# A new order of work on three engines in the odd layer of an encoder

## The chip, the cores and the metric

The kernel runs on one core of one Trainium2 chip, in one launch. The metric is the device time of that launch in microseconds (us), lower is better. A run gives one time; a profiled execution gives a trace as well, with its own span from the first to the last instruction. TensorE (PE) multiplies, ScalarE (ACT) and VectorE (DVE) work on its results, and SyncE (SP) issues the transfers.

## The reference

The program is a two-layer encoder trunk over x of 512 x 1024, float32: an even layer (differential attention beside a gated recurrence), then the odd layer, then a final RMS norm. The change touches only the odd layer:

```python
h = rmsnorm(x, norm_w)
qc, kc, vc, gc = split_cols(h @ w_in, (2048, 256, 256, 2048))
oc = window_gqa_with_sink(qc, kc, vc, sink, cos, sin) * silu(gc)
x = x + oc @ w_out
```

The attention has 32 query heads of 64 features that share 4 key heads; each query sees keys at most 128 positions away, and each head has a learned sink logit in its softmax:

```python
s = q @ k.T / 8, masked to |i - j| <= 128
m = max(max(s), sink)
p = exp(s - m); p = p / (sum(p) + exp(sink - m))
o = p @ v
```

## The kernel before

All float32 products are made from split parts: a matrix w becomes `w_hi` (rounded, by ScalarE: `high`) and `w_lo` (the rest, by VectorE: `low`), and each product is three matmuls, lines 73 to 75. Everything is kept transposed, features on the partitions, 512 tokens along the free dimension.

The odd layer has eight iterations `h` (`HEADS`), and each has two half-steps, `half` 0 and 1. A half-step treats two query heads: their scores against the window, in four tiles `t` of 128 queries, for the two heads `a` side by side. Iteration 0 is written out, iterations 1 to 6 are a loop, iteration 7 is written out again. Each engine runs its own program, written out by hand in `half_step`, and they meet only at semaphores; each engine works strictly in the order written. That order is what the change alters.

What a half-step does, by the names in the code:

- `proj(h, n)` on TensorE: 24 matmuls that project 128 columns of `w_in`. n = 1 and 3 give queries, 2 and 4 give gates. Two banks `PB` take them in turns. Each is issued as two parts of 12, with other work between. `rotate` (VectorE, six operations) reads a query projection, `silu` (ScalarE, line 1523) a gate projection into `gate[:, half]`; both free the bank.
- `scores(t)` on TensorE into banks `S`; `maxima(t)` on VectorE (two reductions, line 1648, and a small operation, line 1652); `soft_max(t)` on ScalarE (line 1483, exp, two times); `turns(t)`: TensorE transposes the probabilities into banks `T` (line 1309); `high_turn(t)` (ScalarE, line 1490) and `low_turn(t)` (VectorE, line 1659) split them into `probsT`; `values(t)` multiplies with v into bank `O` (line 1323). There is one `probsT`, so `values(t)` must wait for `low_turn(t)`. Tile 3 of a half-step is finished in the next one, which begins with `turns(.., 3)`.
- After two tiles `swap_halves` (ScalarE, lines 1502 and 1503) and `add_halves` (VectorE, lines 1690 and 1692) put the two heads' results together.
- The row sums: `exp_sink` and `weigh` make 1 / sum, `spread_weight` (ScalarE, line 1495) widens it to 64 columns, `turn_weight` (TensorE, line 1333) transposes it into bank `W`, `apply_weight` multiplies by the gate (line 1697), `scale_y` by the result (line 1704). `high_y` and `low_y` split this into y.
- `out_tile(j)` on TensorE: six matmuls of the output projection of the iteration before, into the same single bank `W`; `add_out` on VectorE (line 1716) adds it to the residual `xT` and frees W. There are four tiles per half-step, and `out_tile(j)` waits for `add_out` of tile j - 1. Iteration 0 has none.
- The weights: SP loads n = 3, 4, 5, 6 of each iteration into four slots (`load`), and the out weights (`load_out`). `high` and `low` split n = 3 to 6 for use in this and the next iteration, `high_out` and `low_out` the out weights. A load waits for the low part that last read its slot; loads 5 and 6 stand in SP's queue behind the moves of the rotated queries of half 1, the out weights behind these.

Silu needs another function table on ScalarE than exp, and each change of table is an instruction of 1.28 us. In the odd layer before, these loads stand right in front of the activation that needs them, at lines 1523 and 1483.

The order in a half-step before, where it matters: ScalarE ends a half-step with `soft_max` 3, `exp_sink` and the silu of the gate that TensorE made in this half-step. VectorE makes a `low` between `add_halves` and `add_out` of tile 1, and a second one behind `add_out` of tile 2. TensorE has `turn_weight` between the two parts of its first projection.

## Time and profile before

| | us |
|---|---|
| three runs | 1277.93, 1285.24, 1282.14 |
| median | 1282.14 |
| the profiled execution | 1286.09 |
| its span | 1284.3 |
| TensorE busy | 1166.4 (91%) |
| VectorE busy | 965.6 (75%) |
| ScalarE busy | 653.3 (51%) |
| mean granted TensorE clock | 0.971 of full |

The odd layer's half-steps fill the stretch from about 805 to 1250 us of the span. The profiled execution's own time is 1.8 us above its span, and 4 us above the median of the three runs. Busy shares are means over stages with different limits; a busy TensorE is one that has a matmul in flight.

### The profile page before, as it was taken

What the parts mean: (1) busy time and instruction counts of PE and PEld (TensorE: products, weight loads), DVE (VectorE), ACT (ScalarE), POOL (GpSimd) and SP (SyncE); (2) the same over time, 40 slices, a digit from 0 to 9 for tenths busy, and PEclk for the clock granted to TensorE, in tenths of its full rate; (3) what the DMA queues carried; (4) which work ended last, traced back from release to release, by engine and by line L of the source; (5) the groups of instructions that cost most, each with busy time, mean ns of one, the idle gap of its engine ahead of it and who ended that gap; (6) DMA issues with size and microseconds to landing.
All of it is one profiled execution on the core that took longest, in us unless ns stands there. A gap on an engine that the chain in (4) does not pass through costs nothing. (4 is left out here: it accounts for less than half of the span.)

```text
span 1284.3 us, 18420 instructions
## 1 busy us (share of the span) xinstructions
PE 1166.4 (91%) x5708; PEld 931.0 (72%) x5708; DVE 965.6 (75%) x1891; ACT 653.3 (51%) x1246; POOL 0.2 (0%) x4
## 2 busy tenths in 40 slices
PE   5989999999999999999999769889898888989975
PEld 3767778777787787787777547767777777777754
DVE  6677779778788797787787857567777777777764
ACT  5364463553645545535445433565556565555652
POOL 0000000000000000000000000000000000000000
PEclk8999999999999999999999879989999999999998
DMA  6521522315215115233151005412132321213201
GB/s 184 148 66 50 144 69 67 114 49 131 65 43 137 49 50 146 65 80 100 49 131 34 17 25 128 131 51 82 50 101 72 89 82 50 83 49 88 70 7 66
DMA packets 131096, 103.06 MB, mean 80 GB/s; under 512 B 5360, under 2 KB 116336, under 8 KB 131056
## 3 DMA queue, kind: packets, MB, share of 16 engines
q1 hardware_dynamic: 131056, 102.54, 29.2%
q8 instruction: 23, 0.38, 0.1%
q14 instruction: 17, 0.14, 0.0%
HBM read 77.36 MB, written 2.10 MB: 62 GB/s over the span
## 5 line engine op out<-in xcount | busy, mean ns | idle before, releaser
L73 PE MATMUL bank_proj<-hH,w_hi 128*128 128x512 f32 x576 | 229.9, 399 | 4.3 <-DVE hL L139 4.3
L75 PE MATMUL bank_proj<-hH,w_lo 128*128 128x512 f32 x576 | 225.8, 392 | 0.0
L74 PE MATMUL bank_proj<-hL,w_hi 128*128 128x512 f32 x576 | 225.5, 391 | 0.0
L73 PEld LDWEIGHTS bank_proj<-hH,w_hi 128*128 128x128 f32 x576 | 109.0, 189 | 26.5 <-issue 5.1
L75 PEld LDWEIGHTS bank_proj<-hH,w_lo 128*128 128x128 f32 x576 | 108.8, 189 | 23.7
L74 PEld LDWEIGHTS bank_proj<-hL,w_hi 128*128 128x128 f32 x576 | 109.1, 189 | 21.6
L73 PE MATMUL bank_odd_proj<-hH,w_hi 128*128 128x512 f32 x288 | 118.8, 412 | 5.1 <-DVE hL L139 4.4
L1483 ACT ACTIVATE probs<-bank_odd_score,small 128x256 f32<-128x256 f32 (+1 forms) x128 | 66.4, 524 | 105.7 <-DVE small L1652 105.4
L74 PE MATMUL bank_odd_proj<-hL,w_hi 128*128 128x512 f32 x288 | 114.2, 396 | 0.0
L75 PE MATMUL bank_odd_proj<-hH,w_lo 128*128 128x512 f32 x288 | 114.2, 396 | 0.0
L968 DVE TENSOR_TENSOR w_lo<-w_raw,w_hi 128x1024 fp32r<-128x1024 f32 x73 | 89.0, 1220 | 20.1 <-ACT w_hi L565 20.0
L565 ACT ACTIVATE w_hi<-w_raw 128x1024 fp32r<-128x1024 f32 x75 | 78.6, 1051 | 39.9 <-DMA w_raw<-in_w_in_even 36.3
L612 ACT ACTIVATE probs<-bank_score,small 128x512 f32<-128x512 f32 x64 | 43.5, 684 | 95.5 <-DVE small L818 95.5
L1490 ACT ACTIVATE probsT<-bank_odd_turn 128x256 fp32r<-128x256 f32 (+1 forms) x128 | 49.0, 435 | 74.0 <-PE bank_odd_turn L1309 74.0
L1659 DVE TENSOR_TENSOR probsT<-bank_odd_turn,probsT 128x256 fp32r<-128x256 f32 (+1 forms) x128 | 56.9, 486 | 37.4 <-ACT probsT L1490 37.3
L465 PE MATMUL bank_score<-scaled 128*128 128x128 f32 x448 | 61.0, 287 | 10.5 <-DVE attT L984 8.9
L73 PE MATMUL bank_odd_wide<-y,o_hi 128*128 128x512 f32 x112 | 49.4, 441 | 22.5 <-DVE xT L1716 21.8
L668 ACT ACTIVATE scaled<-decay 128x1024 f32<-128x1024 f32 x32 | 33.9, 1059 | 70.4 <-PE bank_score L465 68.6
L465 PEld LDWEIGHTS bank_score<-scaled 128*128 128x128 f32 x448 | 57.7, 200 | 16.2 <-issue 7.1
L73 PEld LDWEIGHTS bank_odd_proj<-hH,w_hi 128*128 128x128 f32 x288 | 55.7, 193 | 16.4 <-DVE hL L139 5.5
L1294 PE MATMUL bank_odd_score<-ks,qs 128*128 128x256 f32 (+1 forms) x256 | 65.1, 359 | 0.0
L75 PEld LDWEIGHTS bank_odd_proj<-hH,w_lo 128*128 128x128 f32 x288 | 55.0, 191 | 12.3
(229 smaller groups left out, 2439.8 us busy)
## 6 DMA issues: line engine op xcount, KB each, us to landing
w_raw<-in_w_in_even SPq DMA_DIRECT2D x72, 512.0 KB, 4.4
w_raw<-in_w_in_odd SPq DMA_DIRECT2D x36, 512.0 KB, 4.5
qs<-parts SPq DMA_DIRECT2D x96, 128.0 KB, 2.3
ks<-parts SPq DMA_DIRECT2D x40, 256.0 KB, 4.2
o_raw<-in_w_out_even SPq DMA_DIRECT2D x16, 512.0 KB, 4.9
o_raw<-in_w_out_odd SPq DMA_DIRECT2D x14, 512.0 KB, 6.5
out<-w_raw SPq DMA_DIRECT2D x4, 512.0 KB, 2.7
mixT<-in_x SPq DMA_DIRECT2D x2, 512.0 KB, 5.5
```

Source lines behind the costliest of these rows:

```text
L73: pe.matmul(out, hi, moving_hi, start=start, stop=False)
L74: pe.matmul(out, hi, moving_lo, start=False, stop=False)
L75: return pe.matmul(out, lo, moving_hi, start=False, stop=stop)
L465: mm = pe.matmul(S[l % 2][:, c * P:(c + 1) * P], scaled[:, l % 2, 0, c * P:(c + 1) * P], scaled[:, l % 2, 1, c * P:(c + 1) * P], start=Tru ...
L565: act.activation(w_hi[s][:], w_raw[s][:], ACT.Copy).then_inc(w_high.sem, 1)
L612: act.activation(probs[:, c], S[c][:], ACT.Exp, bias=neg_max[:, i:i + 1], scale=SCALE, accum_out=row_sum[:, i:i + 1]).then_inc(S[c].free.s ...
L668: act.activation(scaled[:, l % 2], buf(l)[:, :, :], ACT.Exp).then_inc(near_exp.sem, 1)
L968: dve.tensor_tensor(w_lo[s][:], w_raw[s][:], w_hi[s][:].bitcast(F32), ALU.subtract).then_inc(w_low.sem, 1)
L1294: mm = pe.matmul(at, query, keys, start=part == 0, stop=False)
L1483: act.activation(probs[:, t % 2, a, 0:n * P], S[a][:, 0:n * P], ACT.Exp, bias=neg_max[:, i:i + 1], scale=SCALE, accum_out=row_sum[:, i:i + ...
L1490: act.activation(probsT[:, 0, 0:n, a], chunked(T[a][:, 0:n * P]), ACT.Copy).then_inc(probs_high[a].sem, 1)
L1659: dve.tensor_tensor(probsT[:, 1, 0:n, a], chunked(T[a][:, 0:n * P]), probsT[:, 0, 0:n, a].bitcast(F32), ALU.subtract).then_inc(T[a].free.s ...
```

## The change

It moves calls within `half_step` on the three engines. No operation of the attention or the projections is added or left out. What moves:

- TensorE: `turn_weight` from between the two parts of the first projection to behind `scores` 1.
- ScalarE: the silu of a gate moves from the end of its half-step to the next one, behind `swap_halves`; an explicit load of the exp table stands behind `high_turn` 0. `high_y` 0 moves to the beginning of the next iteration's half 0. Both `high_out` stand in front of `soft_max` 0 in half 0; `high` 4 and `high` 5 stand in front of `soft_max` 0 in half 1; `high` 3 and `high` 6 stand behind `soft_max` 1.
- VectorE: `apply_weight` and `scale_y` move behind `maxima` 1. `low` 4 and `low` 5 stand at the beginning of half 1, around `add_halves`; `low` 3 and `low` 6 stand between `add_out` 2 and `add_out` 3. Nothing but `add_halves` is left between `add_out` 0 and 1. `maxima` 3 comes before `low_turn` 2. `rotate` comes before `low_y` 1.

```diff
--- before.py
+++ after.py
@@ -1378,11 +1378,12 @@
                     proj(h, n, 0)
                 if not first:
                     values(h_before, before, 3, group if half else group_before)
-                    turn_weight(h_before, before, turn_of(half, outs))
                 if project:
                     proj(h, n, 1)
                 turns(h, half, 0)
                 scores(h, half, 1)
+                if not first:
+                    turn_weight(h_before, before, turn_of(half, outs))
                 if project:
                     proj(h, n + 1, 0)
                 values(h, half, 0, group)
@@ -1517,9 +1518,8 @@
 
                 bank, use = bank_of(n)
                 act.wait_ge(bank.full.sem, bank.full.at(h, use))
-                if not zeroth:
-                    if W.free.due(h, turn_of(n // 4, True)):
-                        act.wait_ge(W.free.sem, W.free.at(h, turn_of(n // 4, True)))
+                if n == 2 and not zeroth:
+                    act.wait_ge(W.free.sem, W.free.at(h, turn_of(0, True)))
                 act.activation(gate[:, half], bank[:], ACT.Silu).then_inc(bank.free.sem, 1)
 
             nrm.highs(act)
@@ -1549,37 +1549,37 @@
 
             def half_step(h, half, zeroth, last):
                 before, h_before = 1 - half, (h if half else h - 1)
-                n = 3 + 2 * half
                 first, outs = zeroth and not half, not zeroth and not half
                 if not first:
                     high_turn(h_before, before, 3)
                 if outs:
+                    high_y(h - 1, 0)
                     high_out(h - 1, 0)
+                    high_out(h - 1, 1)
+                if half:
+                    high(h, 4)
+                    if not last:
+                        high(h, 5)
                 soft_max(h, half, 0)
                 if not first:
                     spread_weight(h_before, before)
-                if outs:
-                    high_out(h - 1, 1)
-                if not first:
                     swap_halves(h_before, before, 1)
-                if not last or not half:
-                    high(h, n)
+                    silu(h_before, 4 - 2 * half, half, zeroth)
                 high_turn(h, half, 0)
+                act.preload_act_table_set(EXP_LOG)
+                soft_max(h, half, 1)
+                if not half:
+                    high(h, 3)
+                elif not last:
+                    high(h, 6)
                 if outs:
                     high_y(h - 1, 1)
-                soft_max(h, half, 1)
-                if not last or not half:
-                    high(h, n + 1)
                 high_turn(h, half, 1)
                 soft_max(h, half, 2)
                 swap_halves(h, half, 0)
                 high_turn(h, half, 2)
                 soft_max(h, half, 3)
                 exp_sink(h, half)
-                if not (last and half):
-                    silu(h, 2 + 2 * half, 1 - half, zeroth and not half)
-                if half:
-                    high_y(h, 0)
 
             def iteration(h, zeroth, last):
                 half_step(h, 0, zeroth, last)
@@ -1590,6 +1590,7 @@
                 iteration(h, False, False)
             iteration(HEADS - 1, False, True)
             high_turn(HEADS - 1, 1, 3)
+            high_y(HEADS - 1, 0)
             spread_weight(HEADS - 1, 1)
             swap_halves(HEADS - 1, 1, 1)
             high_y(HEADS - 1, 1)
@@ -1742,44 +1743,45 @@
             def half_step(h, half, zeroth, last):
                 before, h_before = 1 - half, (h if half else h - 1)
                 first, use = zeroth and not half, turn_of(half, not zeroth)
-                lows = not (last and half)
+                out = lambda j: zeroth or add_out(h, [4 * half + j], 5 * half + 2 + j)
                 if not first:
                     low_turn(h_before, before, 3)
                 maxima(h, half, 0)
                 if not first:
                     weigh(h_before, before)
-                if not half and not first:
-                    low_y(h - 1, 0)
+                if half:
+                    low(h, 4)
+                elif not first:
                     low_out(h - 1, 0)
                     low_out(h - 1, 1)
+                    low_y(h - 1, 0)
                 if not first:
                     add_halves(h_before, before, 1)
+                if half and not last:
+                    low(h, 5)
+                low_turn(h, half, 0)
+                maxima(h, half, 1)
+                if not first:
                     apply_weight(h, before, use)
                     scale_y(h_before, before, h, use)
-                low_turn(h, half, 0)
-                maxima(h, half, 1)
+                if not (last and half):
+                    rotate(h, 2 * half + 1)
                 if not half and not first:
                     low_y(h - 1, 1)
-                if not (last and half):
-                    rotate(h, 2 * half + 1)
                 low_turn(h, half, 1)
                 maxima(h, half, 2)
-                if not zeroth:
-                    add_out(h, range(4 * half, 4 * half + 1), 5 * half + 2)
+                out(0)
                 add_halves(h, half, 0)
-                if lows:
-                    low(h, 3 + 2 * half)
-                if not zeroth:
-                    add_out(h, range(4 * half + 1, 4 * half + 2), 5 * half + 3)
+                out(1)
+                maxima(h, half, 3)
                 low_turn(h, half, 2)
-                maxima(h, half, 3)
+                out(2)
                 shift_sink(h, half)
-                if not zeroth:
-                    add_out(h, range(4 * half + 2, 4 * half + 3), 5 * half + 4)
-                if lows:
-                    low(h, 4 + 2 * half)
-                if not zeroth:
-                    add_out(h, range(4 * half + 3, 4 * half + 4), 5 * half + 5)
+                if not half:
+                    low(h, 3)
+                elif not last:
+                    low(h, 6)
+                out(3)
 
             def iteration(h, zeroth, last):
                 half_step(h, 0, zeroth, last)
```

## Rows read from the trace of the kernel before

A row of a timeline is: start in us, duration in us, engine, line, operation, tiles, count, and in brackets the idle time before it with what ended it.

**Rows 1.** TensorE's waits, 835 to 1254 us: line and tile, releaser, total us, times, longest.

```profile
PE bank_odd_wide L73 <- DVE xT L1716: 21.8, 31, 1.2
PE bank_odd_wide L1333 <- ACT spread L1495: 12.1, 10, 1.7
PE bank_odd_out L1323 <- DVE probsT L1659: 7.1, 5, 2.9
PE bank_odd_turn L1309 <- ACT probs L1483: 2.3, 3, 1.0
```

**Rows 2.** Timeline of TensorE over one iteration.

```profile
1000.85 0.60 PE L1309 MATMUL bank_odd_turn<-eye,probs 128*128 128x128 f32 x4
...
1008.40 0.60 PE L1309 MATMUL bank_odd_turn<-eye,probs 128*128 128x128 f32 x4
...
1009.82 0.47 PE L73 MATMUL bank_odd_proj<-hH,w_hi 128*128 128x512 f32 x1
...
1015.87 0.82 PE L1309 MATMUL bank_odd_turn<-eye,probs 128*128 128x128 f32 x6
...
1022.67 0.23 PE L1296 MATMUL bank_odd_score<-band,eye_b 128*128 128x128 bf16 x1
1024.08 0.50 PE L73 MATMUL bank_odd_wide<-y,o_hi 128*128 128x512 f32 x1 [1.18 <-DVE xT L1716]
...
1025.59 0.88 PE L1323 MATMUL bank_odd_out<-probsT,v 128*128 128x256 f32 x6
1026.88 0.47 PE L73 MATMUL bank_odd_wide<-y,o_hi 128*128 128x512 f32 x1 [0.41 <-DVE xT L1716]
...
1028.34 0.60 PE L1309 MATMUL bank_odd_turn<-eye,probs 128*128 128x128 f32 x4
...
1034.52 0.63 PE L1333 MATMUL bank_odd_wide<-eye,spread 128*128 128x128 f32 x4 [1.62 <-ACT spread L1495]
...
1057.76 0.60 PE L1309 MATMUL bank_odd_turn<-eye,probs 128*128 128x128 f32 x4
```

**Rows 3.** Timeline of ScalarE, same iteration, around the two changes of table.

```profile
999.47 1.28 ACT L1523 ACT_TABLE_LOAD   x1
1000.77 0.60 ACT L1523 ACTIVATE gate<-bank_odd_proj 128x512 f32<-128x512 f32 x1
...
1031.54 1.28 ACT L1483 ACT_TABLE_LOAD   x1 [0.63 <-DVE small L1652]
...
1034.27 1.05 ACT L1474 ACTIVATE o_hi<-o_raw 128x1024 fp32r<-128x1024 f32 x1
```

**Rows 4.** Timeline of VectorE in half 1 of that iteration.

```profile
1016.92 1.02 DVE L1659 TENSOR_TENSOR probsT<-bank_odd_turn,probsT 128x384 fp32r<-128x384 f32 x2 [1.70 <-ACT probsT L1490]
...
1022.08 1.23 DVE L1723 TENSOR_TENSOR w_lo<-w_raw,w_hi 128x1024 fp32r<-128x1024 f32 x1
1023.34 0.69 DVE L1716 TENSOR_TENSOR xT<-xT,bank_odd_wide 128x512 f32<-128x512 f32 x1
1023.95 1.02 DVE L1659 TENSOR_TENSOR probsT<-bank_odd_turn,probsT 128x384 fp32r<-128x384 f32 x2
1024.88 0.75 DVE L1648 TENSOR_REDUCE small<-bank_odd_score 128x1 f32<-128x256 f32 x2
1025.66 0.16 DVE L1652 SCALAR_TENSOR_TENSOR small<-small,neg_sink 128x2 f32<-128x2 f32 x1
```

**Rows 5.** TensorE's waits, 860 to 1227.6 us.

```profile
PE bank_odd_wide L1333 <- ACT spread L1495: 9.2, 7, 1.6
```

**Rows 6.** SP's issues around load 5, and the page's row on landing.

```profile
1048.18 1.09 SPq L1190 DMA_DIRECT2D w_raw<-in_w_in_odd  x2
...
w_raw<-in_w_in_odd SPq DMA_DIRECT2D x36, 512.0 KB, 4.5
```

**Rows 7.** One stretch: busy us (instructions) of five engines, granted clock, DMA share, GB/s.

```profile
853.00:863.00 10.00, 7.89 (x29) 6.43 (x30) 7.11 (x17) 6.95 (x15) 0.00 (x0) 0.66 0.02 5
```

**Rows 8.** Table loads of the even layer's preload, by line.

```profile
L719 ACT ACT_TABLE_LOAD x8 | 10.3, 1283 | 0.1
```

## The prediction, made before the changed kernel was run

> **What bounds the kernel now.** I read four views. The page's busy line first: TensorE is busy 91% of the span, so what can be won is its idle time and its slow clock. Then the waits of TensorE over the part that the change touches: four waits, 21.8 + 12.1 + 7.1 + 2.3 = 43.3 us [rows 1]. Then TensorE in order of time for one iteration, to see where in a half-step each gap falls, and ScalarE and VectorE at the same places [rows 2 to 4].
>
> I call the start of `turns(.., 3)` time 0 of a half-step. Half 1 starts at 1000.85 and ends at 1028.34 (27.5 us), half 0 ends at 1057.76 (29.4 us) [rows 2]. Their TensorE work is the same; the 1.9 us between them is mostly one gap, 1.62 us before the transposes of the spread sums. Both halves have a gap of 1.18 us before `out_tile` 2 and of 0.41 before `out_tile` 3. These gaps count from the modelled end of a matmul; the next one may start before that end. So I reckon from start to start, which makes a gap some 0.17 us more: half 1's first out matmul at 1024.08 could have started at 1022.73, 0.06 behind the last of `scores` 3 (1022.67).
>
> **Gap 1, the spread sums (half 0).** ScalarE converts one out weight, loads the exp table (1031.54, after waiting for VectorE), does `soft_max` 0 and then the spread [rows 3]. TensorE has only half a projection and `values` 3 to cover that. After the change `turn_weight` stands behind `scores` 1. Working forward for the new half 0, by the durations in these rows and the starts in the same view: `high_turn` 3 at 0.42 to 0.95; `high_y` 0.5, to 1.5; two `high_out` of 1.05 (1034.27), to 3.6; `soft_max` 0 takes 0.9, to 4.5, with no table load in it; spread 0.5, to 5.0; the two halves of the swap 0.8, to 5.8; table load 1.28 and silu 0.5, to 7.6. `turn_weight` now comes at 8.6: without it, and with the two halves of the projection set together, `turns` 0 starts at 7.2 (in half 1 it is at 1008.40 with 0.35 us of those transposes ahead), and `scores` 1 end 1.4 later (1008.40 to 1009.82). The spread is 3.6 us early. The wait goes whole: 9.2 us in the seven half-0 steps from 860 to 1227.6 [rows 5].
>
> **What of the silu hides.** It frees the bank that `proj(n+1)` writes, at 9.0; silu ends at 7.6, so 1.3 us are over. It also stands before `high_turn` 0, whose input is there at 7.2 + 0.41 = 7.6 (two transposes' time and the signal): no delay, and no slack. In half 1 `high` 4 and `high` 5 take the place of the out weights (ends 3.1), `soft_max` 0 ends at 4.0, the swap waits for `values` 3 until 4.6 as before and the silu ends near 7.2. The exp load, now behind `high_turn` 0, lies at 8.2 to 9.5; `soft_max` 1 can start at about 9.9, since VectorE must reduce `scores` 1 first. It costs nothing. As many loads as before (two a half-step), each at a place where ScalarE idled.
>
> **Gaps 2 and 3, the low parts.** `out_tile` 2 waits for `add_out` 1 on VectorE, and that stands behind a 1.23 us low part (1022.08, then 1023.34) [rows 4]. With `low` gone from there, `add_out` 1 starts at 1022.1, and its result is seen at 1022.83, against the 1022.73 at which TensorE could go on. Gap 2 shrinks to 0.1. Next `values` 2 needs `low_turn` 2, which now stands behind `maxima` 3. From 1022.7: two reductions 0.75 (the second not before 1022.95, when its scores are whole), the small operation 0.16 and its start delay, to 1023.75; `low_turn` 2 takes 0.93 (1023.95 to 1024.88), seen by TensorE at 1024.70. `out_tile` 2 ends its issue at 1022.83 + 1.51 = 1024.34 (1.51 is 1024.08 to 1025.59). So a **new wait of 0.36 us** per half-step appears before `values` 2; bounds: 0, if the reductions overlap more, and 0.91, if all of `maxima` 3 were exposed; I take 0.36, for its terms are rows. `add_out` 2 then runs from 1024.7 to 1025.4, before `values` 2 has issued at 1025.42, so gap 3 goes whole, and `out_tile` 3 takes 1.46: the half-step ends at 1026.88 where it ended at 1028.34 [rows 2], **1.46 us** sooner. The one low part left runs at 24.5 to 25.7 of the half-step; the next projection wants it at 27, and `add_out` 3, behind it, has its input at 26.2.
>
> **VectorE's first part.** Half 0: `low_turn` 3, `maxima` 0 and `weigh` to 3.0, two `low_out` of 1.2, to 5.3, `low_y` to 5.9; then the swap is just ready, `add_halves` to 6.8, `low_turn` 0 at 8.06 (`turns` 0 + 0.83), `maxima` 1 to 9.9. `apply_weight` and `scale_y`, 1.55 with their wait, now sit between this and `rotate` (4.0), then `low_y` 0.6: 16.1. `low_turn` 1 can start at 15.05 + 1.05 = 16.1 (1015.87 to 1016.92 is that 1.05) [rows 2, 4]. Exactly on time. In half 1 there is no `low_y`, and the old idle of 1.70 at 1016.92 becomes 0.55. I charge 0, with bounds 0 and 0.5 us per half 0.
>
> **Weight loads.** SP's waits are for `rotate` and for low parts that all end no later than now, so the loads start within 1 us of the same place. But `high` 5 is wanted sooner: load 5 is issued 2.8 us behind the rotation's end (1048.18), so at 18.3, lands 4.5 later at 22.8 [rows 6], and is read at 28.0. 5 us are over.
>
> **First and last iteration.** In iteration 0 no output tiles cover VectorE; the 7.1 and 2.3 us of [rows 1] lie mostly there. `values` 2 waits 2.9 twice; its chain (softmax 2, swap, `add_halves`, a low part) loses 1.23 and gains `maxima` 3, 0.91: 0.3 better twice. `turns` 3 no longer waits for `soft_max` 3 (0.5), nor `turn_weight` for the spread (0.3). About 1.4 us. TensorE ran at the lower of its two levels for part of this: over 853 to 863 its granted clock is 0.66 of full, after such a wait [rows 7]. Whether a wait of 2.6 instead of 2.9 spares that is open: between 0 and 5 us gained; I take 1. The last half-step has no projections: there silu and both loads fall into a chain of latencies, to about 7.2 for `high_turn` 0, but VectorE's `maxima` 1 comes where it came (8.9), as it had `apply_weight` and `scale_y` ahead before. With the spread's 1.7 partly gone and this, 0.5 gained (bounds: 2 lost, 2 gained).
>
> **Sum.** From 860 to 1227.6 there are six half-1 steps and seven half-0 steps: 13 x 1.46 = 19.0 for gaps 2 and 3 less the new wait; gap 1, 9.2, and start to start 7 x 0.17 = 1.2 more; half 0's first `out_tile` waits stay. That is 29.4. Then 1.4 + 1 + 0.5. Together **32 us**. The profiled execution took 1286.1 (span 1284.3), so 1254; it stands 4 us above the median of the three runs (1282.1). Against the median: **1250**.
>
> The Trainium skill (ScalarE: Activation LUTs, What ACT_TABLE_LOAD costs) counts a drain of about 1.38 us with every 1.28 us load. The trace shows the silu starting 1.30 us after its load began, with nothing between, at 999.47 and 1000.77 [rows 3], so it isn't in my sum; it is the second rival.
>
> **Rivals.**
> (a) VectorE becomes the bound. For: in the new half 0 nothing is over before `low_turn` 1, and from there `maxima` 2, `soft_max` 2, the swap, `add_halves` and `add_out` 1 follow without slack to `out_tile` 2. Each microsecond late comes back whole. Against: half 1 has 0.55 over. At 0.8 us in 13 half-steps, 10 us: 1260.
> (b) A table load costs more than its row when ScalarE has work queued on either side. For: in the old order its neighbours were often waits. Against: the silu's load shows none [rows 3]. Were 1.3 us paid behind each, the silu ends at 8.9 in half 0 and `high_turn` 0 is 1.3 late; in half 1 0.3 after slack: 7 x 1.3 + 6 x 0.3 = 11 us, 1261. This is what the Trainium skill's drain would make.
> (c) A load that is not wanted appears: the first exp of the loop gets one of its own, since silu ran before it elsewhere. The Trainium skill (ScalarE: Activation LUTs, Table sets: the hidden batching unit) says that a compiler pass puts a load before every activation that needs one. Against: the even layer loads by an explicit preload (line 719) in each of its 8 turns, and its exps at the loop's top show no load of their own [rows 8]. Price: 1.28 before `soft_max` 0 of half 0 pushes silu and `high_turn` 0 by as much, 7 x 1.28 = 9: 1259.
> (d) **Slower**: ScalarE stands at `high` 5 for a weight that hasn't landed, with `soft_max` 0 of half 1 queued behind it, and so spread, swap, silu and the whole half-step. It was behind `soft_max` before, in a gap. The slack is 5.2 us and an iteration gains 4.5 (29.4 over 6.5 of them), so it decides from a load 9.7 us late, 14 us instead of 4.5 to land; at 17 us the loss is 2.8 net in each of 7 iterations: 1282 + 20 = 1302. Against it: nothing else is on the queue then but the small q moves and the out weights behind it.
> (e) The gaps are only passed on, TensorE's idle returning elsewhere: within 0.5% (6 us, about what this kernel's measurement can tell from no change). It would need 2 us of new wait per half-step (26 over 13); no step above is over by so much.
>
> **Chances.** Forecast 0.70 (own range 1243 to 1257), (a) 0.12, (b) 0.05, (c) 0.05, (d) 0.03, (e) 0.05. All of the forecast, (a), (b) and (c) are faster by over 0.5%, 0.92; same 0.05; slower 0.03. The low end takes the slow clock of the first iteration as spared (4 us more) and the new wait at nothing (13 x 0.36 = 5, of which I count half, since both ends rarely meet): 1243. The high end reaches past (a) to (c), 1264.
>
> **What would show it.** The transposes from `spread` with no wait before them; no wait of TensorE on `xT` over 0.3 us; a new one on `probsT` before `values` 2 of 0.1 to 0.5 us, some 13 times; half-steps of 26.0 to 26.3 us, both alike; table loads still 16 and 16, now under lines of silu and preload, the first exp with one of its own at most once. Wrong: waits on `xT` of 1 us left, or the projection waiting for the silu, or half 0 longer than half 1 by over 0.5.

## The result, and the profile after

| | before | after |
|---|---|---|
| median of four runs, us | 1282.01 | 1248.3 |
| lowest and highest | 1277.93 to 1285.24 | 1245.95 to 1249.27 |
| the profiled execution, and its span | 1286.09, 1284.3 | 1248.77, 1247.0 |
| from TensorE's first `scores` to the end of the span | 475.97 | 444.27 |

The ratio is 0.9736, with a 95% interval of 0.9705 to 0.9767: 33.7 us by the medians, where 32 were forecast. The two spans differ by more, 37.3 us, and 5.65 us of that lie ahead of the first `scores` (808.35 against 802.70), in code that the change does not touch. The part that it touches gave 31.7. In the tables below I therefore count from the first `scores` of each trace.

TensorE's waits in the changed kernel from 800 to 1220 us, which is its odd layer but for the very end; columns as in [rows 1]:

```profile
PE bank_odd_out L1323 <- DVE probsT L1660: 12.9, 21, 2.5
PE bank_odd_turn L1309 <- ACT probs L1484: 3.3, 4, 1.0
PE bank_odd_wide L1333 <- ACT spread L1496: 1.0, 1, 1.0
PE bank_odd_wide L73 <- DVE xT L1717: 0.6, 4, 0.2
```

[Rows 1] begin at 835 us, 27 us into the odd layer. Over the part that corresponds to the one above, 805 to 1254 us, the kernel before has the same two first lines, 3.1 us on `probs`, and on `probsT`:

```profile
PE bank_odd_out L1323 <- DVE probsT L1659: 10.4, 7, 2.9
```

The 21.8 us on `xT` of [rows 1] are 0.6; the 12.1 on the spread are 1.0, one wait behind the last half-step. What grew is the wait on `probsT`, 10.4 to 12.9. Of its 21 waits, 14 are the new short one before `values` 2 (0.17 to 0.30 us each); the other 7, in the first iteration and the last half-step, have their counterparts in the kernel before.

TensorE over one iteration, half 0 from 1007.17 to 1033.21 and the half 1 ahead of it from 981.13 (a row: start us, us, engine, line, operation, tiles, count, idle before and its releaser):

```profile
981.13 0.60 PE L1309 MATMUL bank_odd_turn<-eye,probs 128*128 128x128 f32 x4
...
989.69 0.61 PE L1333 MATMUL bank_odd_wide<-eye,spread 128*128 128x128 f32 x4
...
1002.95 0.23 PE L1296 MATMUL bank_odd_score<-band,eye_b 128*128 128x128 bf16 x1
1003.10 0.50 PE L73 MATMUL bank_odd_wide<-y,o_hi 128*128 128x512 f32 x1
...
1004.98 0.96 PE L1323 MATMUL bank_odd_out<-probsT,v 128*128 128x256 f32 x6 [0.23 <-DVE probsT L1660]
```

```profile
1005.77 0.40 PE L73 MATMUL bank_odd_wide<-y,o_hi 128*128 128x512 f32 x1
...
1007.17 0.60 PE L1309 MATMUL bank_odd_turn<-eye,probs 128*128 128x128 f32 x4
...
1015.73 0.61 PE L1333 MATMUL bank_odd_wide<-eye,spread 128*128 128x128 f32 x4
...
1031.03 0.95 PE L1323 MATMUL bank_odd_out<-probsT,v 128*128 128x256 f32 x6 [0.17 <-DVE probsT L1660]
...
1033.21 0.60 PE L1309 MATMUL bank_odd_turn<-eye,probs 128*128 128x128 f32 x4
```

Both half-steps take 26.04 us, where [rows 2] had 27.5 and 29.4. The transposes of the spread sums (989.69, 1015.73) wait for nothing. `out_tile` 2 starts at 1003.10, 0.15 behind the last of `scores` 3, `values` 2 waits 0.23 (0.17 in half 0), and `out_tile` 3 follows at 1005.77 without a wait.

ScalarE in half 0, for [rows 3], and VectorE at the places of [rows 4]:

```profile
1008.65 2.01 ACT L1475 ACTIVATE o_hi<-o_raw 128x1024 fp32r<-128x1024 f32 x2
1010.55 0.47 ACT L1484 ACTIVATE probs<-bank_odd_score,small 128x256 f32<-128x256 f32 x1
...
1011.45 0.64 ACT L1496 ACTIVATE spread<-small 128x512 f32<-128x512 f32 x1
...
1012.91 1.28 ACT L1523 ACT_TABLE_LOAD   x1
1014.21 0.60 ACT L1523 ACTIVATE gate<-bank_odd_proj 128x512 f32<-128x512 f32 x1
1014.70 0.66 ACT L1491 ACTIVATE probsT<-bank_odd_turn 128x256 fp32r<-128x256 f32 x2
1015.38 1.28 ACT L1569 ACT_TABLE_LOAD   x1
1017.03 0.58 ACT L1484 ACTIVATE probs<-bank_odd_score,small 128x384 f32<-128x384 f32 x1 [0.37 <-DVE small L1653]
```

```profile
997.20 1.02 DVE L1660 TENSOR_TENSOR probsT<-bank_odd_turn,probsT 128x384 fp32r<-128x384 f32 x2 [0.72 <-ACT probsT L1491]
...
1002.36 0.69 DVE L1717 TENSOR_TENSOR xT<-xT,bank_odd_wide 128x512 f32<-128x512 f32 x1
1002.96 0.75 DVE L1649 TENSOR_REDUCE small<-bank_odd_score 128x1 f32<-128x256 f32 x2
...
1003.82 1.01 DVE L1660 TENSOR_TENSOR probsT<-bank_odd_turn,probsT 128x384 fp32r<-128x384 f32 x2
...
1022.44 0.69 DVE L1710 TENSOR_TENSOR y<-gated,y 128x512 fp32r<-128x512 f32 x1
1023.24 1.02 DVE L1660 TENSOR_TENSOR probsT<-bank_odd_turn,probsT 128x384 fp32r<-128x384 f32 x2
```

`high_turn` 0 takes over from the silu at 1014.70, which is 7.53 us into the half-step (from 1007.17), with no idle time, as worked out (7.6). The exp load (1015.38) stands 8.2 us into it and `soft_max` 1 9.9, both as forecast. `maxima` 3 (1002.96) comes before `low_turn` 2 (1003.82). `low_turn` 1 comes at 1023.24 behind `low_y` at 1022.44 with nothing between (16.07, forecast 16.1); in half 1 there is an idle 0.72 instead of the 1.70 of [rows 4]. The function table is loaded 16 times for the silus and 16 times by the explicit preload, and one first exp has a load of its own:

```profile
L1523 ACT ACT_TABLE_LOAD x16 | 20.5, 1283 | 0.3
L1569 ACT ACT_TABLE_LOAD x16 | 20.5, 1283 | 0.3
...
L1484 ACT ACT_TABLE_LOAD x1 | 1.3, 1283 | 0.0
```

Where the 31.7 us came from, by stretches that begin and end with `turns(.., 3)`:

| stretch | before | after | gained | forecast |
|---|---|---|---|---|
| iteration 0, from the first `scores` | 47.70 | 46.25 | 1.45 | 2.4 |
| 13 half-steps up to the last | 371.59 | 340.49 | 31.10 | 29.4 |
| the last half-step | 22.51 | 23.39 | -0.88 | 0.5 with the end |
| from its `turns` 3 to the end | 34.17 | 34.14 | 0.03 | |
| sum | 475.97 | 444.27 | 31.70 | 32.3 |

### The profile page after: what moved, and what is told of

Same layout as the page of the kernel before. It is cut to its first block and busy times, and to the rows that moved or that the text cites. A ratio compares the mean times of both kernels' runs of the same rounds, so it can differ in the third digit from the quotient of the medians.

```text
span 1247.0 us, 18415 instructions
## 1 busy us (share of the span) xinstructions
PE 1158.3 (93%) x5708; PEld 926.6 (74%) x5708; DVE 961.7 (77%) x1891; ACT 653.4 (52%) x1247; POOL 0.2 (0%) x4
## 5 line engine op out<-in xcount | busy, mean ns | idle before, releaser
L968 DVE TENSOR_TENSOR w_lo<-w_raw,w_hi 128x1024 fp32r<-128x1024 f32 x73 | 88.8, 1217 | 19.8 <-ACT w_hi L565 19.8
L1660 DVE TENSOR_TENSOR probsT<-bank_odd_turn,probsT 128x256 fp32r<-128x256 f32 (+1 forms) x128 | 57.0, 485 | 28.3 <-ACT probsT L1491 27.5
L1323 PEld LDWEIGHTS bank_odd_out<-probsT,v 128*128 128x128 f32 x320 | 45.9, 192 | 23.0 <-issue 16.5
```

Source lines behind the costliest of these rows:

```text
L968: dve.tensor_tensor(w_lo[s][:], w_raw[s][:], w_hi[s][:].bitcast(F32), ALU.subtract).then_inc(w_low.sem, 1)
L1323: mm = pe.matmul(at, value, probsT[:, part, j].rearrange("p a q -> p (a q)"), start=j == 0 and part == 0, stop=j == n - 1 and part == 1)
L1660: dve.tensor_tensor(probsT[:, 1, 0:n, a], chunked(T[a][:, 0:n * P]), probsT[:, 0, 0:n, a].bitcast(F32), ALU.subtract).then_inc(T[a].free.s ...
```

## The experiments

Ten kernels ran, each beside the kernel before on the same chip. Two theories stood against each other throughout. One, by slack: an edit is worth what it takes off the path that ends last, and what it puts on it, and much of it lies beside other work. The other, by gaps: an edit is worth the gap that it was made for.

The two half-steps in the table are those of one iteration near 1000 us.

| kernel | median, us | half 1, half 0, us | iteration 0 | 13 half-steps | last half-step |
|---|---|---|---|---|---|
| before | 1282.0 | 27.5, 29.4 | 47.70 | 371.59 | 22.51 |
| changed | 1248.3 | 26.04, 26.04 | 46.25 | 340.49 | 23.39 |
| e1, `turn_weight` back | 1254.2 | 26.18, 27.02 | 46.22 | 346.71 | 23.45 |
| e2, `turn_weight` alone | 1278.9 | 28.05, 28.51 | 47.06 | 370.64 | 23.02 |
| e3, low parts back | 1269.6 | 27.27, 27.28 | 49.79 | 356.62 | 23.47 |
| e4, `low_turn` 2 first | 1245.2 | 25.96, 26.05 | 45.03 | 338.71 | 22.83 |
| e5, silu back | 1246.1 | 26.09, 26.04 | 46.22 | 340.74 | 20.63 |
| e6, filler on VectorE | 1250.1 | 26.04, 26.46 | 46.24 | 343.07 | 22.18 |
| e7, one more table load | 1255.6 | 26.04, 27.26 | 46.20 | 347.17 | 23.15 |
| e8, round trip filled | 1233.1 | 25.2, 25.6 | 42.11 | 330.71 | 23.02 |
| e10, last silu back | 1246.7 | 26.02, 26.02 | 46.20 | 340.32 | 20.62 |
| e9, e8 and the last half | 1231.4 | 25.2, 25.6 | 42.09 | 330.63 | 20.96 |

**e1: `turn_weight` back between the parts of the projection.** On the changed kernel:

```diff
                     values(h_before, before, 3, group if half else group_before)
+                    turn_weight(h_before, before, turn_of(half, outs))
...
                 scores(h, half, 1)
-                if not first:
-                    turn_weight(h_before, before, turn_of(half, outs))
```

> The changed kernel, but turn_weight stands between the two parts of the first projection again, as before the change. Nothing else is undone. Theory (slack): the table load is no longer ahead of the spread, so the spread is ready 4.9 us into half 0 and 4.4 into half 1, and TensorE comes to it at 4.4: a wait of 0.5 to 0.7 us in half 0 and under 0.15 in half 1, 7 x 0.6 + 6 x 0.1 = 5 us: 1253. Rival (the move of turn_weight is what removed gap 1): the wait of 1.6 us per half 0 comes back whole, 11 us: 1259 to 1260.

1254.23 us, ratio to before 0.9799 (0.9772 to 0.9827); 6.2 us more than the changed kernel over the 13 half-steps. The spread is waited for by 0.53 us in half 0, not by the 1.62 of [rows 2], as the theory by slack has it. What neither had: in half 0 a second wait, before `out_tile` 1, and a half 1 that is 0.14 us longer.

```profile
1012.58 0.63 PE L1333 MATMUL bank_odd_wide<-eye,spread 128*128 128x128 f32 x4 [0.53 <-ACT spread L1495]
...
1023.30 0.82 PE L1309 MATMUL bank_odd_turn<-eye,probs 128*128 128x128 f32 x6
...
1027.57 0.47 PE L73 MATMUL bank_odd_wide<-y,o_hi 128*128 128x512 f32 x1 [0.30 <-DVE xT L1716]
```

From `turns` 0 to `turns` 1 it is 7.46 us again (1015.84 to 1023.30), in the changed kernel 7.90 (1014.29 to 1022.19). With the transposes between them, VectorE has 0.4 us more for its chain from `low_turn` 0 to `low_turn` 1, which was exactly on time. So the move of `turn_weight` is worth 6.2 us of the 13 half-steps. By the waits in half 0, 0.53 + 0.17 from start to start is 7 x 0.7 = 5 of them, an estimate, and a high one, since the first half 0 takes 28.08 us in both kernels. I put the rest down to the stretch in which VectorE was tight and which the move lengthens; no run shows that part by itself. What took the wait from 1.62 to 0.53 is the load and the order on ScalarE together; no run divides these two.

**e2: `turn_weight` alone, on the kernel before.**

```diff
-                    turn_weight(h_before, before, turn_of(half, outs))
...
                 scores(h, half, 1)
+                if not first:
+                    turn_weight(h_before, before, turn_of(half, outs))
```

> The kernel before, with one edit of the change alone: turn_weight behind scores 1. Theory (slack): gap 1 goes (1.8 us from start to start per half 0), but VectorE's apply_weight, which still stands before low_turn 0 and maxima 1, now waits for the transposes until 9.0 us into the half-step, so low_turn 0 ends at 11.2 instead of 9.1, rotate ends at 16.4 in half 1 and 17.0 in half 0, and low_turn 1 is 0.3 and 0.9 us late; that comes back before out_tile 2. 7 x (1.8 - 0.9) - 6 x 0.3 = 4.5 us gained: 1277.5. Rival (the edit is worth its gap): 7 x 1.7 = 12 us gained, 1270.

1278.92 us, ratio 0.9989 (0.9974 to 1.0005): no clear change. The 13 half-steps are 0.95 us shorter. A steady half 0 gained 0.8 where 0.9 were expected, half 1 lost 0.5 instead of 0.3. The wait on `xT` from 860 to 1220 us, columns as in [rows 1]:

```profile
PE bank_odd_wide L73 <- DVE xT L1717: 30.7, 39, 1.4
```

The spread's 9.2 us of [rows 5] are gone, and the wait on `xT` took nearly all of them (21.8 in [rows 1]): `apply_weight`, still ahead of `low_turn` 0, holds VectorE until the late transposes are done. By itself the edit is worth nothing. That its partner on VectorE (`apply_weight` behind `maxima` 1) would be enough to free its 6.2 us is likely by e1, but the two were not run as a pair.

**e3: the low parts back in their gaps.** On the changed kernel:

```diff
                 add_halves(h, half, 0)
+                if not (last and half):
+                    low(h, 3 + 2 * half)
                 out(1)
...
+                if not (last and half):
+                    low(h, 4 + 2 * half)
                 out(3)
```

with `low` 4 and 5 gone from the beginning of half 1, and on ScalarE `high(h, 3 + 2 * half)` and `high(h, 4 + 2 * half)` both behind `soft_max` 1.

> The changed kernel, with the low parts back in their old gaps on VectorE (one between add_halves and add_out 1, one before add_out 3), and the two high parts they need both behind soft_max 1 on ScalarE. maxima 3 stays before low_turn 2. Theory (slack): add_out 1 is 1.23 us later, TensorE had 0.1 us over it, all behind it is late by the same: half-steps of 27.2 instead of 26.04, 13 x 1.15 = 15 us: 1263. Rival (gaps 2 and 3 are both the low parts' work and the new wait stays on top): 13 x 1.8 = 24 us: 1272.

1269.55 us, ratio 0.9915 (0.9888 to 0.9941). A steady half-step is 1.27 us longer (27.30 on the mean, 26.03 in the changed kernel), about one low part of [rows 4], 16.1 us over the 13, and iteration 0 is 3.5 us longer, which the expectation left out; together 19.8 from the first `scores` on. The short wait before `values` 2 stayed as it was (waits from 860 to 1208 us):

```profile
PE bank_odd_wide L73 <- DVE xT L1712: 15.9, 16, 1.2
PE bank_odd_out L1323 <- DVE probsT L1655: 2.7, 13, 0.2
```

This is the largest single part of the change: 19.8 of 31.7 us. With the 6.2 of e1 that is 26.0; what makes up the other 5.7 no run shows.

**e4: `low_turn` 2 before `maxima` 3 again.**

```diff
-                maxima(h, half, 3)
                 low_turn(h, half, 2)
+                maxima(h, half, 3)
                 out(2)
```

> The changed kernel with one pair exchanged on VectorE: low_turn 2 before maxima 3 again. Theory (slack): the new wait before values 2 (0.2 us from the modelled end, 0.3 from start to start) goes; soft_max 3 is 0.9 us later, still 1 us before turns 3 need it; add_out 2 comes 0.1 late at most. Half-steps of 25.75 instead of 26.04, 13 x 0.27 = 3.5 us gained: 1245. Rival (VectorE is the bound here, so the order is indifferent and the wait moves to out_tile 3): same, 26.0 per half-step.

1245.18 us, ratio 0.9732 (0.9708 to 0.9757). The wait before `values` 2 went, but a half-step behind the first gained 0.04 us on the mean, not 0.27: the theory by slack, as I had filled it in, failed, and the first rival is right about the half-steps. The wait moved to `out_tile` 3. TensorE and VectorE at that place:

```profile
999.39 0.50 PE L73 MATMUL bank_odd_wide<-y,o_hi 128*128 128x512 f32 x1
...
1000.88 0.88 PE L1323 MATMUL bank_odd_out<-probsT,v 128*128 128x256 f32 x6
1001.92 0.47 PE L73 MATMUL bank_odd_wide<-y,o_hi 128*128 128x512 f32 x1 [0.16 <-DVE xT L1717]
```

```profile
999.25 1.01 DVE L1660 TENSOR_TENSOR probsT<-bank_odd_turn,probsT 128x384 fp32r<-128x384 f32 x2
...
1001.09 0.69 DVE L1717 TENSOR_TENSOR xT<-xT,bank_odd_wide 128x512 f32<-128x512 f32 x1
```

`add_out` 2 (1001.09) can't start before `out_tile` 2's last matmul is done, and takes 0.69; so two out tiles can't follow each other within about 2.5 us (999.39 to 1001.92), while the tile and `values` 2 between them issue in 2.2. That round trip through the single bank W holds `out_tile` 3. VectorE's own work would hold it as well: `maxima` 3 is done at 1001.12, the last matmul of `out_tile` 2 at 1001.04, so at this place the two limits can't be told apart. At `out_tile` 1 of half 0, which waits 0.16 us too, they can: VectorE is free 0.1 us before `add_out` 0 starts (1021.71, the last matmul of `out_tile` 0 ends at 1021.68), and the two tiles stand 2.49 us apart (1020.05 to 1022.54). The median is 3.1 us below the changed kernel's. In the traces 3.7 us are gained, and they lie in iteration 0 (1.2), in the 13 half-steps (1.8, over half of it in the first of them, which runs partly at the lower clock) and in the last half-step (0.6).

**e5: the silu back at the end of its half-step.**

```diff
-                    silu(h_before, 4 - 2 * half, half, zeroth)
                 high_turn(h, half, 0)
-                act.preload_act_table_set(EXP_LOG)
...
                 exp_sink(h, half)
+                if not (last and half):
+                    silu(h, 2 + 2 * half, 1 - half, zeroth and not half)
```

The silu's own wait for W stands as in the kernel before.

> The changed kernel, with the silu back at the end of its own half-step and the exp table loaded where soft_max 0 needs it; all else as changed. Theory (slack): in half 0 soft_max 0 comes 1.3 us later, behind the load, the swap ends at 7.1 instead of 5.8, but high_turn 0 has its input only at 7.5 and turn_weight comes at 8.6: nothing on TensorE's path moves, half-steps of 26.0 to 26.1, 1248 to 1250. Rival (the silu's move is what took the load off the spread's path, and is worth its 1.3 us per half 0): 7 x 1.3 = 9 us more, 1257.

1246.14 us, ratio 0.9734 (0.9698 to 0.9771), its interval over that of the changed kernel. The 13 half-steps are 0.25 us longer, so the move of the silu, taken from the finished order, is worth nothing there: the first theory held and the rival's 9 us did not come. But the last half-step takes 20.63 us instead of 23.39. ScalarE in that half-step, in the changed kernel and in e5:

```profile
1194.28 1.28 ACT L1523 ACT_TABLE_LOAD   x1
1195.58 0.60 ACT L1523 ACTIVATE gate<-bank_odd_proj 128x512 f32<-128x512 f32 x1
1196.07 0.65 ACT L1491 ACTIVATE probsT<-bank_odd_turn 128x256 fp32r<-128x256 f32 x2
```

```profile
1193.77 0.66 ACT L1491 ACTIVATE probsT<-bank_odd_turn 128x256 fp32r<-128x256 f32 x2
```

`high_turn` 0 comes 6.6 us into the half-step in the one and 5.8 in the other (from 1189.44 and 1187.98): with no projection for TensorE, silu and load stand in a chain of latencies. But that chain is the smaller part of the difference, as e10 shows below.

**e6: a filler before `rotate`.**

```diff
                 if not (last and half):
+                    dve.tensor_reduce(filler[:, half:half + 1], rope[:, 0], AX_X, ALU.max)
                     rotate(h, 2 * half + 1)
```

> The changed kernel with one more operation on VectorE in front of each rotate, a reduction of 512 columns whose result nobody reads, some 0.65 us. Theory (VectorE's chain to low_turn 1 is exactly on time in half 0): half 1 has 0.72 us over and stays at 26.0; half 0 has 0.15 to 0.2 over and becomes 26.5, 7 x 0.47 = 3.3 us: 1251.5. Rival (VectorE is the bound throughout, so each half-step pays): 13 x 0.65 = 8.5 us: 1257. Rival (TensorE alone is the bound): nothing, 1248.

1250.14 us, ratio 0.9753 (0.9718 to 0.9787). The filler takes 0.68 us. Half 0 grew by 0.42 us, half 1 by nothing, as the theory by slack had it (0.47 and 0); over the 13 half-steps it is 2.6 us, where 3.3 were expected. So the idle 0.72 us in half 1 are real slack, and half 0 has some 0.25.

**e7: one more table load before `soft_max` 0 of half 0.**

```diff
                     high_out(h - 1, 1)
+                    act.preload_act_table_set(EXP_LOG)
```

> The changed kernel with one more load of the exp table on ScalarE, in front of soft_max 0 of half 0 (1.28 us, 7 times on the path from 860 us on). Theory (nothing is over on the way silu, high_turn 0, low_turn 0, rotate, low_turn 1): half 0 grows by 1.1 to 1.3 us, half 1 not; 7 x 1.2 = 8.5 us: 1257. Rival (a load costs a drain beside its row): 7 x 2.5 = 17 us, 1265. Rival (ScalarE is idle half the time, so a load hides): 1248.

1255.63 us, ratio 0.9805 (0.9768 to 0.9841). Half 0 takes 27.26 us, 1.22 more, the row's 1.28 less a little; half 1 stays at 26.04. 6.7 us over the 13 half-steps, where 8.5 were expected: the first half 0 of them, which runs in part at the lower clock, grew by nothing (27.74 us, in the changed kernel 28.08). So this load costs its row and nothing beside it, and in a steady half 0 it comes back whole. TensorE's `turns` 3 at the two ends of a half 0 (the half 1 behind it ends at 1063.11):

```profile
1009.82 0.60 PE L1309 MATMUL bank_odd_turn<-eye,probs 128*128 128x128 f32 x4
...
1037.08 0.60 PE L1309 MATMUL bank_odd_turn<-eye,probs 128*128 128x128 f32 x4
```

**e8: work for TensorE in W's round trip.** On top of e4, the two projections of a half-step cut differently, and the silu table loaded ahead of `high_turn` 0:

```diff
-                    proj(h, n, 1)
+                    proj(h, n, tiles=range(4, 7))
                 turns(h, half, 0)
                 scores(h, half, 1)
+                    proj(h, n, tiles=range(7, 8))
                     turn_weight(h_before, before, turn_of(half, outs))
...
-                    proj(h, n + 1, 1)
+                    proj(h, n + 1, tiles=range(4, 6))
                 turns(h, half, 1)
...
                 values(h, half, 1, group)
+                    proj(h, n + 1, tiles=range(6, 7))
...
                 values(h, half, 2, group)
+                    proj(h, n + 1, tiles=range(7, 8))
...
+                    act.preload_act_table_set("silu_and_others")
+                high_turn(h, half, 0)
+                if not first:
                     silu(h_before, 4 - 2 * half, half, zeroth)
-                high_turn(h, half, 0)
```

> A further version: e4 (low_turn 2 before maxima 3), and the eighth part of the first projection moved behind scores 1, the seventh and eighth part of the second behind values 1 and values 2, so that TensorE has work while VectorE adds an out tile and frees the single bank W; on ScalarE the silu table is loaded ahead of high_turn 0 and the silu comes behind it. Theory (since e4 what is left is the round trip of W, 0.3 us twice a half-step, and VectorE's chain, which the earlier turns 0 pulls forward by 0.7 us): half-steps of 25.5 to 25.6 instead of 25.97, 13 x 0.42 = 5.5 us: 1240. Rival (VectorE's chain is the bound in half 0 and does not move): half 1 gains 0.4, half 0 nothing, 1243. Rival (the later silu makes the second projection wait for its bank): 1246 or more.

1233.06 us, ratio 0.9621 (0.9587 to 0.9654); the interval is wholly below that of the changed kernel. TensorE has no wait at all between 860 and 1176 us. Half 0 takes about 25.6 us and half 1 25.17 to 25.2, and the 13 half-steps 8.0 us less than in e4, where 5.5 were expected. Half 0 gained 0.4 us and half 1 0.8, so neither rival holds. The work in W's round trip, the earlier `turns` 0 and the load ahead of `high_turn` 0 came together; no run takes them apart. The matmuls between `values` 2 and `out_tile` 3:

```profile
996.17 0.88 PE L1324 MATMUL bank_odd_out<-probsT,v 128*128 128x256 f32 x6
996.89 0.40 PE L73 MATMUL bank_odd_proj<-hH,w_hi 128*128 128x512 f32 x1
...
997.60 0.40 PE L73 MATMUL bank_odd_wide<-y,o_hi 128*128 128x512 f32 x1
```

Iteration 0 gained 2.9 more against e4, which the expectation had left out; with it the median came 7 us below the 1240 that were expected. There too TensorE has work in the gaps, and its clock was granted more: 0.98 of full over that iteration, where the changed kernel and e4 both had 0.94 (columns as in [rows 7]; the changed kernel first).

```profile
802.70:848.95 46.25, 38.87 (x218) 31.95 (x217) 30.73 (x68) 25.91 (x63) 0.00 (x0) 0.94 0.41 111
```

```profile
803.94:846.05 42.11, 37.82 (x218) 30.28 (x216) 30.82 (x68) 25.61 (x63) 0.00 (x0) 0.98 0.45 123
```

**e10: the last silu back, on the changed kernel.** The silu of the last iteration's half 1 stands at the end of half 0 again, and no explicit load in the last half-step:

```diff
-                    silu(h_before, 4 - 2 * half, half, zeroth)
+                    if not (last and half):
+                        silu(h_before, 4 - 2 * half, half, zeroth)
...
                 exp_sink(h, half)
+                if last and not half:
+                    silu(h, 2, 1)
```

> The changed kernel, but in the last iteration alone the silu stands at the end of half 0 again, and the exp table is loaded by soft_max 0 of half 1. Theory (the silu's move costs where no projection covers ScalarE: in the changed kernel the last half-step takes 23.4 us against 22.5 before, in e5 20.6): the last half-step 20.5 to 21, 2.5 us gained: 1246. Rival (that difference is the granted clock's phase in the two traces): last half-step 22.5 to 23.5, 1248.

1246.65 us, ratio 0.9728 (0.971 to 0.9746). The last half-step takes 20.62 us, as in e5, against 23.39, with the rest of the kernel as it was. The medians differ by 1.65 us and their intervals overlap, so the difference is read from the traces.

Of the 2.8 us, only 0.33 lie ahead of `turns` 1, where the silu stands: `turns` 1 come 9.68 us into the half-step in the changed kernel and 9.35 in e10. The other 2.44 lie behind it, where both have the same work. The stretch from `turns` 1 to the next `turns` 3 in the changed kernel, in e6 (whose last half-step has the same order as the changed kernel's) and in e10:

```profile
1199.12:1212.83 13.71, 13.24 (x62) 10.60 (x63) 7.62 (x17) 5.59 (x17) 0.00 (x0) 0.79 0.01 2
```

```profile
1204.54:1217.03 12.49, 12.02 (x63) 9.63 (x64) 7.64 (x17) 5.59 (x17) 0.00 (x0) 0.88 0.00 1
```

```profile
1202.11:1213.38 11.27, 10.83 (x62) 8.57 (x63) 7.54 (x17) 5.58 (x17) 0.00 (x0) 1.00 0.01 2
```

The time goes with the granted clock, 0.79, 0.88 and 1.00. So the rival, the clock, accounts for most of the difference. It is not chance alone: with the silu in the last half-step seven traces have 22.18 to 23.47 us for it, without it three have 20.62 to 20.96 (e5, e10, e9). In the changed kernel TensorE waited 2.49 us shortly before that stretch, in e10 no wait there is over 1.51, and the low clock came and went ahead of `turns` 1. That the longer wait brought the lower clock into the full stretch is my reading; e6 shows that the same order can lose 1.2 us less.

**e9: e8 with the last iteration as in e10,** and `high` 4 and `low` 4 of the last half-step behind `soft_max` 1 and before the last `add_out`:

```diff
-                if half:
+                if half and not last:
                     high(h, 4)
...
+                elif last:
+                    high(h, 4)
...
+                else:
+                    low(h, 4)
                 out(3)
```

> e8 with the last iteration ordered for latency: its silu at the end of half 0 as in e10, and high 4 and low 4 (the last out weight) out of the way, behind soft_max 1 and before the last add_out. Theory: the last half-step, 23.0 in e8, becomes 20.5 to 21.5; 1230 to 1231. Rival (as for e10): same as e8, 1233.

1231.35 us, ratio 0.9616 (0.9595 to 0.9638). Its last half-step is 2.06 us shorter than in e8. It has the lowest median of the study, 17 us below the changed kernel's; against e8 the intervals overlap.

## Why the prediction was right

**Gap 1 and the silu.** The forecast times in half 0 were 3.6 for the end of `high_out`, 4.5 for `soft_max` 0, 7.6 for the silu and 8.6 for `turn_weight`; the rows have 3.4, 4.3, 7.5 and 8.6. The wait went whole. The working did not say which part of the change empties it; e1 divides it: with the new order on ScalarE and `turn_weight` at its old place 0.5 of the 1.6 us is left, and on the kernel before the move alone gives nothing (e2). That the silu's move itself is worth nothing in these half-steps was not in the working, which only called it free; e5 shows it.

**Gaps 2 and 3.** Right in both size and mechanism: 1.46 us per half-step was the forecast, 1.50 the mean of the six half-1 steps (27.54 to 26.04). The new wait came at its place with 0.17 to 0.23 us from the modelled end, 0.33 to 0.39 from start to start (forecast 0.36). e3 gives the low parts' share directly, one low part per half-step. Another order does not save it: e4.

**VectorE's chain.** "Exactly on time" in half 0 and 0.55 over in half 1: the rows have 0 idle and 0.72, and e6 and e7 show that what is added on this chain in half 0 comes back at 0.42 of 0.68 and 1.22 of 1.28 us, and in half 1 at nothing (e6). Rival (a) was thus a real danger that did not fall due.

**Rivals (b), (c).** e7 prices a load at its row, which disposes, in this kernel, of the drain of 1.38 us that the Trainium skill (ScalarE: Activation LUTs, What ACT_TABLE_LOAD costs) counts beside it. The load of e7 is of the table that is active already; at a real change of table the trace leaves no room for a drain either, for the silu starts 1.30 us behind the start of its load (1012.91, 1014.21). Of (c), one load appeared, in the written-out iteration 0 where a silu stands right ahead; the loop has none. Its price, 7 x 1.28 = 9 us, was right for each turn and a little high in sum: e7 has 1.22 in a steady half 0 and 6.7 us in all.

**Rivals (d), (e).** ScalarE does not stand at `high` 5: in half 1 it follows `high` 4 in one group of 2.01 us with no idle time.

```profile
982.09 2.01 ACT L1470 ACTIVATE w_hi<-w_raw 128x1024 fp32r<-128x1024 f32 x2
```

The idle time did not return elsewhere: TensorE's waits fell from 47.4 us (805 to 1254) to 17.8 (800 to 1220).

**What was off.** The last half-step: I took 0.5 us gained for it and the end, and it lost 0.88, within the bounds given. The forecast's step for it, that silu and loads delay `high_turn` 0 but "`maxima` 1 comes where it came", held: 8.76 us into the half-step, before 8.95. Up to `turns` 1 it is 0.19 us shorter than before. The loss lies behind that, where from `turns` 1 to `turns` 3 it took 13.71 us at a granted clock of 0.79 and before 12.64 at 0.86: the working had no term for the clock there. Nor did it see that without the silu this half-step could have taken 20.6 us (e5, e10).

The 13 half-steps gained 1.7 us more than forecast (31.1, not 29.4). 1.0 of it lies in the first half 0. It went from 31.09 to 28.08 us, though its wait on the spread had been only 0.41, and its granted clock rose from 0.90 to 0.92. Iteration 0 gained 1.45 instead of 2.4: its waits shrank from 9.0 to 7.4 us, where the sum counted 1.4, but the 1 us for the clock did not come. Over iteration 0 the granted clock was 0.96 before and 0.94 after, and over 10 us across its end (848.95) it is 0.66 again, as in [rows 7].

```profile
846.00:856.00 10.00, 8.47 (x35) 7.46 (x36) 7.56 (x16) 6.24 (x17) 0.00 (x0) 0.66 0.15 43
```

So part of the closeness is luck: three errors, +1.7, -0.95 and -1.35 us, add up to -0.6, and leave 31.7 against 32.3. The remaining 2 us between that and the 33.7 of the medians are not explained; unchanged code differs by more from one execution to the next.

## What to carry to other kernels

Write each engine's times down for one period and look for the slack at every meeting point. An order changed on one engine is worth the least slack behind it, not the gap that it empties; so e2's move gave nothing by itself, while taking e3's part out of the finished order cost 20 us. When the waits are gone, ask what else a gap consists of: a single bank that must be written, read and freed sets the distance of its users, and then the remedy is independent work in between, cut small enough to fit (e8). Order the last turn of a loop by itself; what a steady turn hides stands in the open there. And before a difference in such a thin stretch is put down to an order, compare its granted clock: here the clock was most of it (e10).

## What the runs showed of the hardware that was not expected

A table load between two activations cost 1.22 us of a half-step, its row being 1.28, and no more, even with work queued on both sides (e7). The same work from `turns` 1 to `turns` 3 of the last half-step took 11.27 us at a granted clock of 1.00 and 13.71 at 0.79 (e10 and the changed kernel). And code that did not change takes a different time from one execution to the next: TensorE's first `scores` came at 800.85 to 808.35 us in the twelve traces, a spread of 7.5 us, more than several of the effects measured here. Steady half-steps of one kind, read from one trace, agreed to 0.15 us from turn to turn (to 0.06 in the changed kernel), so an effect of a microsecond per iteration was read from the trace and not from the medians.
